# Recurrent heads of a two-model kernel: values, output gate and numerators by token instead of by channel

## The reference, cut to what matters

```python
ML_HEADS, ML_QK_DIM, ML_V_DIM, ML_CHUNK = 4, 128, 256, 128

def mlstm_chunkwise(q, k, v, i_pre, f_pre):
    ...
    # per chunk: C (128 x 256), n (128) and m carried from chunk to chunk
    C_new = decay[..., None, None] * C + jnp.einsum('bhl,bhlk,bhlv->bhkv', w, ks, vs)
    n_new = decay[..., None] * n + jnp.einsum('bhl,bhlk->bhk', w, ks)
    ...
    qk = jnp.einsum('bhctd,bhcsd->bhcts', qc, kc) * dmat
    num = (jnp.einsum('bhcts,bhcsv->bhctv', qk, vc)
           + inter_w[..., None] * jnp.einsum('bhctd,bhcdv->bhctv', qc, C_prev))
    den = jnp.sum(qk, axis=-1) + inter_w * jnp.einsum('bhctd,bhcd->bhct', qc, n_prev)
    h = num / jnp.maximum(jnp.abs(den), jnp.exp(-m_t))[..., None]
    ...

def even_mixer(h, ...):
    p = jnp.einsum('bsd,de->bse', h, w_in)
    ...
    hm = mlstm_chunkwise(ml_q, ml_k, ml_v, ml_i + b_igate, ml_f + b_fgate)
    hm = hm * jax.nn.sigmoid(ml_o)
    hm = rmsnorm(hm, ml_head_g)
    y_b = hm.reshape(B, S, ML_WIDTH) * jax.nn.silu(ml_z)
    y = jnp.concatenate([y_a, y_b], axis=-1)
    return jnp.einsum('bse,ed->bsd', y, w_out)
```

## Time and profile before

| | us |
|---|---|
| median of three runs | 1956.9 |
| the profiled execution | 1957.01 |
| its span, first to last instruction | 1955.2 |
| TensorE busy | 1938.8 |
| VectorE busy | 1064.3 |
| ScalarE busy | 763.0 |
| GpSimd busy | 68.2 |

### The profile page before, as it was taken

One profiled execution on the slowest core, in us unless ns is written; L12 is line 12 of the kernel. 1 busy time (PEld: TensorE's weight loads), 2 busy tenths in 40 slices (PEclk: granted clock), 3 DMA queues, 4 the chain that ended last, 5 costly groups with the idle time before them and its releaser, 6 DMA issues.

```text
span 1955.2 us, 30945 instructions
## 1 busy us (share of the span) xinstructions
PE 1938.8 (99%) x11880; PEld 1690.6 (86%) x11880; DVE 1064.3 (54%) x1612; ACT 763.0 (39%) x1249; POOL 68.2 (3%) x119
## 2 busy tenths in 40 slices
PE   8999999999999999999999999999999999999998
PEld 8888888888888788888899999999999799899886
DVE  5777777666344355542536555565666364444333
ACT  5544443233233233322435554555642243333222
POOL 3000000000011000000100000000000010000000
PEclk9999999999999999999999999999999999999999
DMA  6222222322323332323232222222122233232321
GB/s 173 80 66 74 75 65 55 86 75 75 119 79 109 91 88 86 87 106 102 71 108 76 66 76 76 76 76 76 55 82 83 85 98 97 86 97 87 107 97 54
DMA packets 244002, 167.25 MB, mean 86 GB/s; under 512 B 5293, under 2 KB 231701, under 8 KB 243910
## 3 DMA queue, kind: packets, MB, share of 16 engines
q1 hardware_dynamic: 242224, 160.98, 27.7%
q10 hardware_dynamic: 1286, 4.23, 0.6%
q0 software_dynamic: 400, 0.72, 0.1%
HBM read 163.81 MB, written 2.10 MB: 85 GB/s over the span
## 4 chain that ended last, share of the span: by engine, by line
PE 96%; DVE 2%; ACT 1%; DMA 1%; issue 0%; SPq 0%; POOL 0%; ACTq 0%; DVEq 0%
PE pj L1809 9%; PE pj L1811 9%; PE pj L1810 9%; PE pj L1270 9%; PE pj L1269 9%; PE pj L1271 9%; PE zz L1270 2%; PE zz L1269 2%; PE zz L1271 2%; PE zz L1326 2%; PE tr L1326 2%; PE zz L1328 2%; PE tr L1328 2%; PE pj L1326 2%; PE tr L1327 2%; PE zz L1327 2%
## 5 line engine op out<-in xcount | busy, mean ns | idle before, releaser
L2129 DVE TENSOR_TENSOR w_lo<-raw,w_hi 128x1024 fp32r<-128x1024 f32 x299 | 365.4, 1223 | 298.1 <-ACT w_hi L654 293.5
L654 ACT ACTIVATE w_hi<-raw 128x1024 fp32r<-128x1024 f32 x299 | 314.8, 1054 | 213.8 <-PE tr L1328 139.9
L1809 PE MATMUL pj<-x_hi,w_hi 128*128 128x258 f32 (+1 forms) x1280 | 365.0, 285 | 0.0
L1811 PE MATMUL pj<-x_hi,w_lo 128*128 128x258 f32 (+1 forms) x1280 | 361.7, 283 | 0.0
L1810 PE MATMUL pj<-x_lo,w_hi 128*128 128x258 f32 (+1 forms) x1280 | 361.0, 282 | 0.0
L1269 PE MATMUL pj<-x_hi,w_hi 128*128 128x512 f32 x760 | 305.8, 402 | 1.4 <-DVE zs L2293 1.4
L1270 PE MATMUL pj<-x_lo,w_hi 128*128 128x512 f32 x760 | 300.7, 396 | 0.0
L1271 PE MATMUL pj<-x_hi,w_lo 128*128 128x512 f32 x760 | 298.9, 393 | 0.0
L1810 PEld LDWEIGHTS pj<-x_lo,w_hi 128*128 128x128 f32 x1280 | 241.7, 189 | 0.8
L1809 PEld LDWEIGHTS pj<-x_hi,w_hi 128*128 128x128 f32 x1280 | 241.3, 189 | 0.9
L1811 PEld LDWEIGHTS pj<-x_hi,w_lo 128*128 128x128 f32 x1280 | 241.3, 188 | 0.0
(11 more groups left out here) (622 smaller groups left out, 3544.4 us busy)
## 6 DMA issues: line engine op xcount, KB each, us to landing
raw<-in_l_w_in_dram SPq DMA_DIRECT2D x113, 512.0 KB, 4.0
raw<-in_w_in_dram SPq DMA_DIRECT2D x64, 512.0 KB, 4.0
raw<-in_w_up_gate_dram SPq DMA_DIRECT2D x44, 512.0 KB, 3.8
raw<-in_l_w_out_dram SPq DMA_DIRECT2D x32, 512.0 KB, 3.4
raw<-in_w_down_dram SPq DMA_DIRECT2D x22, 512.0 KB, 3.3
raw<-in_w_proj_conv_dram SPq DMA_DIRECT2D x8, 512.0 KB, 3.8
raw<-in_w_proj_attn_dram SPq DMA_DIRECT2D x8, 512.0 KB, 3.7
raw<-in_w_out_dram SPq DMA_DIRECT2D x8, 512.0 KB, 3.4
```

Source lines behind the costliest of these rows:

```text
L654: act.activation(w_hi[:, slot], raw[:, slot], ACT.Copy).then_inc(hi_done, 1)
L1809: pe.matmul(dst, w_hi[:, slot, k, :], hi[:, k, tok], start=(k == 0), stop=False)
L1811: ins = pe.matmul(dst, w_lo[:, slot, k, :], hi[:, k, tok], start=False, stop=(k == KD - 1))
L2129: dve.tensor_tensor(w_lo[:, slot], raw[:, slot], w_hi[:, slot].bitcast(F32), ALU.subtract).then_inc(lo_done, 1)
```

## The change

- **Values and output gate by token.** `tokens` computes tiles 2 and 3 together, and tiles 4 and 5 together: the 128 tokens of a chunk are stationary and the 256 channels of two weight slots move. A half (`h`) is two chunks and fills one bank; the first half says `half`, the second frees both slots. It waits for both tiles' splits. ScalarE copies the values straight to `m_v` and writes the gate's tanh by token; the value transposes and copies go.
- **Numerators by token** (`ml_num`, `ml_num_inter`): the weighted query-key block of a chunk is stationary and all 258 columns of `m_v` or of the state move. Column 256 is the denominator. The products with `ones` and `m_nb` go, and `m_nb` itself.
- **Floors by token**: exp(-m) becomes a column (`mcol`, `ecol`, four more small transposes at the start), so the row `r_mt` and its spread go, and `gate_rows(r_nm)` moves from ahead of VectorE's attention head 1 into it.
- **Sums of squares** by ScalarE: `Square` with the reciprocal as scale and `accum_out`; `ml_sums` goes.
- **Scaling, then turning**: VectorE multiplies the 1024 columns of `m_g` by reciprocal and rstd in one operation, and `turn_y` transposes the result (eight transposes) where `ml_spread` stood. VectorE's output is then one operation for each half instead of two.
- In head 0, `split(M_0 + 8)` moves on VectorE from behind the keys' activation to ahead of the state, `split(M_0 + 6)` behind the last softmax, and `turn_o(h7)` goes to bank `tt`. In `o_free` the third bank waits for `y` instead of the mean.

```diff
-        m_cvin, m_to = turns(("m_cvin", [P, 2, T + 4]), ("m_to", [P, 2, T]))
+        m_cvin, m_to = turns(("m_cvin", [P, 2, T + 4]), ("m_to", [P, NT, 2 * P]))
...
-        m_kd, m_sq, m_y = turns(("m_kd", [P, 2, NT, P]), ("m_sq", [P, 2, T]), ("m_y", [P, 2, T]))
-        m_vT, m_h = turns(("m_vT", [P, 2, T]), ("m_h", [P, 2, T]))
+        m_kd, m_y = turns(("m_kd", [P, 2, NT, P]), ("m_y", [P, 2, T]))
+        m_g = sb(w_, "m_g", [P, NT, 2 * P])
...
+            act.wait_ge(G["step"], GATE_STEP["columns"])
+            act.activation(ecol[:], mcol[:], ACT.Exp, scale=-1.0).then_inc(G["step"], 1)
...
-                    act.activation(m_vT0[:, b - 2, :], src, ACT.Copy).then_inc(ML["v"], 1)
+                    act.activation(m_v0[:, (b - 2) * 2:(b - 1) * 2, 0:2 * P], src.rearrange("p (t n) -> p t n", t=2),
+                                   ACT.Copy).then_inc(ML["vtok"], 1)
...
+            def ml_squares(hd):
+                act.wait_ge(ML["recip"], hd + 1)
+                for c in range(NT):
+                    act.wait_ge(ML["g"], hd * NT + (c + 1))
+                    ins = act.activation(m_sq[:, c, :], m_g[:, c, :], ACT.Square, scale=m_r[:, c:c + 1],
+                                         accum_out=q_ms[:, c:c + 1])
+                ins.then_inc(ML["square"], 1)
...
+            def tokens(b, hd, per, h):
+                n = M_0 + b
+                slot, _ = weight_slot(n, hd, per)
+                if h == 0:
+                    pe.wait_ge(lo_done, n + per * hd + NSLOT + 2)
+                for t in (2 * h, 2 * h + 1):
+                    dst = pj[:, (n + h) % 2, (t % 2) * 2 * P:(t % 2 + 1) * 2 * P]
+                    tok = slice(NM + t * P, NM + (t + 1) * P)
+                    for k in range(KD):
+                        wh, wl = w_hi[:, slot:slot + 2, k, :], w_lo[:, slot:slot + 2, k, :]
+                        pe.matmul(dst, x_hi[:, k, tok], wh, start=(k == 0), stop=False)
+                        pe.matmul(dst, x_lo[:, k, tok], wh, start=False, stop=False)
+                        ins = pe.matmul(dst, x_hi[:, k, tok], wl, start=False, stop=(k == KD - 1))
+                if h:
+                    ins.then_inc(tile_done, 2)
+                else:
+                    ins.then_inc(ML["half"], 1)
...
+            def ml_num(c, v):
+                return pe.matmul((rb, aux, zz[:, 1:2], zz)[c][:, 0, 0:VW], m_qw[:, 1, c * P:(c + 1) * P], v[:, c, :],
+                                 start=True, stop=(c == 0))
+            def ml_num_inter(c, state):
+                pe.matmul((rb, aux, zz[:, 1:2], zz)[c][:, 0, 0:VW], m_qw[:, 0, c * P:(c + 1) * P], state[:, c - 1, :],
+                          start=False, stop=True).then_inc(ML["num"], 1)
+            def turn_y(hd):
+                pe.wait_ge(ML["scaled"], hd + 1)
+                for v, dst in enumerate((rb, aux)):
+                    for c in range(NT):
+                        ins = pe.transpose(dst[:, 0, c * P:(c + 1) * P], m_g[:, c, v * P:(v + 1) * P], ident[:])
+                ins.then_inc(ML["yturned"], 1)
...
-            pe.matmul(rb[:, 0, :], ones[:], m_qw[:, 1, :], start=True, stop=True)
...
+            pe.wait_ge(DA["vtok"], HD)
+            ml_num(0, m_v0).then_inc(ML["num"], 1)
+            ml_num(1, m_v0)
+            ml_num(2, m_v0)
             pe.wait_ge(ML["state"], 1)
+            ml_num_inter(1, m_c0)
+            ml_num_inter(2, m_c0)
+            ml_num(3, m_v0)
+            ml_num_inter(3, m_c0)
...
-                proj(0, lambda: ml_spread(hd - 1), at=KD * 3 // 4)
+                proj(0, lambda: turn_y(hd - 1), at=KD * 3 // 4)
...
-                proj(2)
+                tokens(2, hd, 8, 0)
+                pe.wait_ge(ML["conv_in"], hd * 2 + 2)
+                tokens(2, hd, 8, 1)
...
-                pe.matmul(oo[:, 0, :], m_sel[:], r_mt[:], start=True, stop=True).then_inc(ML["spread"], 1)
...
-                proj(3, v_turn(0, rb))
...
-                proj(4, v_turn(1, aux))
+                pe.wait_ge(ML["y"], hd * 2)
+                for t in range(NT):
+                    ins = pe.transpose(aux[:, 0, t * P:(t + 1) * P], m_kT[:, t * P:(t + 1) * P], ident[:])
+                ins.then_inc(ML["kturned"], 1)
+                pe.wait_ge(ML["vtok"], hd * 2 + 1)
...
-                pe.matmul(rb[:, 0, :], ones[:], m_qw[:, 1, :], start=True, stop=True)
-                for c in range(1, NT):
-                    ins = pe.matmul(rb[:, 0, c * P:(c + 1) * P], m_nb[:, c - 1, :], m_qw[:, 0, c * P:(c + 1) * P],
-                                    start=False, stop=(c == NT - 1), skip_group_check=True)
-                ins.then_inc(ML["den"], 1)
-                for v in range(2):
-                    for c in range(NT):
-                        ch = slice(c * P, (c + 1) * P)
-                        ins = pe.matmul(zz[:, v, ch], m_v[:, c, v * P:(v + 1) * P], m_qw[:, 1, ch], start=True,
-                                        stop=(c == 0))
-                        if c:
-                            ins = pe.matmul(zz[:, v, ch], m_c[:, c - 1, v * P:(v + 1) * P], m_qw[:, 0, ch],
-                                            start=False, stop=True)
-                    ins.then_inc(ML["num"], 1)
+                for c in range(NT):
+                    ins = ml_num(c, m_v)
+                    if c:
+                        ml_num_inter(c, m_c)
+                    else:
...
-                ml_sums(hd)
...
-                pe.wait_ge(*((ML["h"], 2 * HM), (ML["zs"], 2 * HM), (ML["mean"], HM), (ML["y"], 2 * HM))[t])
+                pe.wait_ge(*((ML["g"], NT * HM), (ML["zs"], 2 * HM), (ML["y"], 2 * HM), (ML["y"], 2 * HM))[t])
             project(O_0, 2 * KD, 1, y_hi, y_lo, o_free,
                     lambda k: pe.wait_ge(DA["ylo"], HD) if k < KD else pe.wait_ge(ML["ylo"], k - KD + 1),
-                    during=at_point({(0, 3): [lambda: ml_spread(HM - 1)]}),
...
-            dve.wait_ge(G["step"], GATE_STEP["rows"])
-            gate_rows(r_mt, g_mt)
-            gate_rows(r_nm, g_nm)
...
+                    if b == 1 and prev and not prev2:
+                        gate_rows(r_nm, g_nm)
...
+            def ml_recip(hd):
+                dve.wait_ge(G["step"], GATE_STEP["floors"])
+                for c, src in enumerate(nums):
+                    dve.wait_ge(ML["num"], hd * NT + (c + 1))
+                    ins = dve.tensor_tensor(m_r[:, c:c + 1], src[:, 2 * P:2 * P + 1], ecol[:, c, bass.ds(hd, 1)], ALU.max)
+                link(ins)
+                for c, src in enumerate(nums):
+                    ins = dve.scalar_tensor_tensor(m_r[:, c:c + 1], src[:, 2 * P:2 * P + 1], -1.0, m_r[:, c:c + 1],
+                                                   ALU.mult, ALU.max)
+                link(ins)
+                dve.reciprocal(m_r[:], m_r[:]).then_inc(ML["recip"], 1)
+            def ml_gate_o(hd, to):
+                for c, src in enumerate(nums):
+                    if c % 2 == 0:
+                        dve.wait_ge(ML["tanh_o"], hd * 2 + (c // 2 + 1))
+                    dve.scalar_tensor_tensor(m_g[:, c, :], to[:, c, :], 1.0, src[:, 0:2 * P], ALU.add,
+                                             ALU.mult).then_inc(ML["g"], 1)
+            def ml_mean(hd):
+                dve.wait_ge(ML["square"], hd + 1)
+                dve.tensor_scalar(ms[:, 0:NT], q_ms[:], 0.25 / (2 * P), EPS, ALU.mult, ALU.add).then_inc(ML["mean"], 1)
+            def ml_scale(hd):
+                dve.wait_ge(ML["power"], hd + 1)
+                link(dve.tensor_tensor(m_r[:], m_r[:], rstd[:, 0:NT], ALU.mult))
+                dve.tensor_tensor(m_g[:], m_g[:], m_r[:].unsqueeze(2).to_broadcast([P, NT, 2 * P]),
+                                  ALU.mult).then_inc(ML["scaled"], 1)
+            def ml_gate_z(hd, v):
+                dve.wait_ge(ML["tanh_z"], hd * 2 + (v + 1))
+                dve.scalar_tensor_tensor(m_zs[:, v, :], m_tr[:], 1.0, pj[:, (M_0 + 6 + v) % 2, :], ALU.add,
+                                         ALU.mult).then_inc(ML["zs"], 1)
...
-            split(M_0 + 8)
...
+            split(M_0 + 8)
+            ml_state(0, m_c0)```

TensorE in the loop, behind tile 5 (`tokens` or `product`), before:

```order
L1687 MATMUL tr<-m_qw,ones 128x512
L1689 MATMUL tr<-m_qw,m_nb 128x128 x3
L1695 MATMUL zz<-m_qw,m_v 128x128 x2
L1698 MATMUL zz<-m_qw,m_c 128x128
L1695 MATMUL zz<-m_qw,m_v 128x128
L1698 MATMUL zz<-m_qw,m_c 128x128
L1695 MATMUL zz<-m_qw,m_v 128x128
L1698 MATMUL zz<-m_qw,m_c 128x128
L1695 MATMUL zz<-m_qw,m_v 128x128 x2
```

309 lines of the change are left out of this document (117 added, 192 removed).

## The result

| us | before | changed |
|---|---|---|
| median (executions) | 1957.39 (4) | 1943.17 (4) |
| lowest to highest | 1956.72 to 1957.91 | 1941.62 to 1943.34 |
| profiled execution | 1957.01 | 1941.62 |
| its span | 1955.2 | 1939.9 |

The four executions of before are the three behind the forecast's 1956.9 and one more. The ratio of the times is 0.9924, with a 95% interval from 0.9912 to 0.9936: 14.2 us faster by the medians, 15.3 by the two profiled spans. The forecast was 1944.0 us, in a range from 1941.3 to 1947.8.

What follows compares the result with a forecast made beforehand. TensorE was taken as the bound, busy 1938.8 of 1955.2 us. Loop -9.9, head 0 -2.4, first attention heads -1.0 and output projection +0.4 sum to -12.9 us: forecast 1944.0 us, range 1941.3 to 1947.8.

Steps and rivals of the forecast that it cites:

- The loop: Recurrent heads 1 to 3: TensorE's issue time falls by 3.3 us per head, 9.9 for three.
- rival 4: Recurrent heads: more gain from fewer switches and restarts, 0.5 us in each of four, plus 0.9: 1941.1 us; chance 0.09.
- Rival 1: 256-column products in `tokens`: paced by their weight load, +54 us, hence 1998; chance 0.03.
- Chain (b): Last numerator to `turn_y`: about 9 us of work stays hidden behind 15.3 us of TensorE's projection tiles.
- rival 2: Recurrent loop: a new wait in one of the two new chains or at a split, near price 1946.7 us; chance 0.12.
- far bound of 0.69 us: Output chain ahead of `turn_y`: upper price of a VectorE operation on one column, where 0.16 us was taken.
- The far end of rival 2: Ahead of `turn_y`: one-column operations at 0.69, gates, squares and scaling doubled; 3.5 us wait in four heads, 1958, no change.
- Chain (a): Decay mask to state updates: exponentials wait for a later spread; some 2 us of work hidden behind 5.7 us.
- Head 0: Recurrent head woven into the last attention head, led by VectorE: -2.4 us, bounds -3.3 and -1.2.
- The early part: First attention heads: the 1.43 us wait for `zs` goes, small transposes cost 0.3; term -1.0 us, bounds -1.2 and +0.3.

Runs made afterwards that it cites:

- thin sums: Kernel before with two products instead of eight for a recurrent head's sums of squares, first 128 tokens only: 1952.88 us against 1957.97.
- split projections: Kernel before with 2760 projection products of 512 columns split into 5520 of 256, each with its own weight load: 1967.87 us, ratio 1.0053.
- two runs on the gates' rows: Kernel before with rows `r_mt` and `r_nm` written behind `zs`: 1956.73 us; changed kernel with `r_nm` written twice ahead of `zs`: 1945.03 us.

## Why the prediction was right, point by point

**The bound.** TensorE was named as the bound, with starts instead of durations as the price. The doubled `turn_y` (0.87 expected from the earlier trace rows as 0.88) and the thin sums (5.1 us expected and measured) show that it holds for additions and removals.

**The loop** gave 3.75 a head and not 3.3. Two terms gave more than their size. The numerators take 2.86 us from the first to the next projection, not 3.08; but 0.1 of this the next projection product gives back (0.41 to its successor, against 0.32 behind the numerators of before), so the term is some 0.12 better than forecast. And `tokens` costs 0.4, not 0.6: its 192 products take 23.07 us with their restarts, against 96 x 0.236 = 22.7 when restarts are counted on both sides; half of this 0.2 is the price, 0.1184 over the 44 steps for my 0.119, and half the restarts, which I had left out on both sides and of which before has more. One switch less, since the query-key products now follow the spreads, gives another restart of 0.08. The other terms, 1.71 for the sums and 0.88 for `turn_y`, came as forecast, and some 0.07 a head isn't accounted for. This is nearly what rival 4 named for the loop, 0.5 a head from fewer switches and restarts, at a chance of 0.09.

**Rival 1**, a product paced by its weight load, is refuted by the changed kernel (0.118) and by the split projections: 3.2 ns for a pair. The Trainium skill (TensorE: Matmul & The Clock Gate, Back-to-back issue gap) has 81 ns for 128 columns and 131 ns for 512 as sustained spacing, from which the prediction estimated 65 ns more for each pair, 179 us for the 2760 pairs; the run shows 10. The same section's N/2.4 + 2.5 ns for a single gap adds 2.5 ns a pair, 7 us in all, and lies near it.

**Chain (b), rival 2.** The outcome was as forecast, no wait, and the chain took less than I put down: from the last numerator (361.64) to the scaled output (368.83) 7.2 us, where I said about 9, with 0.15 for an operation on one column. That size was no open question: the prediction says that the trace has no operation on one column, but before's trace has one, inside the stretch of the earlier trace rows:

```profile
56.73 0.16 DVE L2367 SCALAR_TENSOR_TENSOR lam<-lame 128x1 f32<-128x1 f32 x1
```

But the slack was misread. I compared the chain with `turn_y` alone, 15.3 us, which leaves 6.3, and so expected nothing from 5 us more. What stands behind the scaling on VectorE, `m_zs`, is wanted sooner, and the slack is 3.5 us in the loop and 2.7 in head 0. The forecast of no wait didn't depend on the size. Only five of the eight one-column operations lie behind the last numerator; the first three start at 359.50, 360.37 and 361.24, one for each numerator as it comes, with VectorE idle for 0.71 us between them. At the far bound of 0.69 us the chain would have grown by an estimated 5 x 0.53 = 2.7 us, which the slack just covers. The far end of rival 2, with gates, squares and scaling doubled too, it would not. Chain (a) never showed a wait in the loop; it wasn't tested by itself.

**Head 0** gave 2.98 and not 2.4. The wait ahead of the updates stayed (0.96 for 0.91), as said. Set back by the 1.45 us that the last attention head came early (VectorE's keys too: they end at 300.71, 302.06 in the earlier trace rows), the marks are: products 302.2 (302.5 forecast), updates 305.2 (305.5), first product with the state 308.4 (308.9), tile 6 310.1 (310.7). So 0.3 us was the products, which did not start later, 0.2 the shorter wait for the state (0.3 instead of 0.6, partly), and 0.1 the start of tile 6 beside the last numerator, which tile 6's first product gives back.

**The early part**: 1.44 gained to 71 us and 0.39 given back by 286 us, against 1.3 and 0.3. The two runs on the gates' rows show the cause of the first. Of the 0.39, the trace gives 0.25 to the four small transposes (TensorE's L1424, from 69.70 us on, 0.06 from start to start): the next tile is 1.59 us ahead of before, not 1.84. Another 0.23 is lost between 271 and 286 us, where head 0's first two `tokens` stand, and 0.08 is won between the two places; no run takes them apart.

**The rest** is not the change: 0.4 us of the profiled difference was there before its first instruction, in a wait for the remainder of the inputs (1.4 and 1.0 us) that is 0.7 to 1.4 in the runs here. Without it the profiled gain is 14.9, against 12.9 forecast; 1.3 of the missing 2.0 are the loop and 0.6 head 0. That the median of 1943.17 lies within 0.9 us of the forecast is in part luck: three of its four executions are on the upper level. The level of 1941.62 lies 2.4 below the forecast and 0.3 inside the range.

## What to carry to other kernels

Price work on a saturated TensorE by distances between starts, restarts included; a product of half the columns then costs half (3 ns more for a pair, at 256 columns), and such sums came out within a seventh here (12.9 of 14.9). For a chain that is to stay hidden, ask not only when its own result is wanted but when the next thing in the same engine's queue is: here an operation that frees an accumulator had to go ahead of a long one whose reader is far away. Before a difference of one or two microseconds is read as an effect, look for stretches at half clock in both executions and compare marks ahead of them.
